# Tile 0's chosen pairs are turned inside the V convolution, z is cut into 16 pieces beside tokens 0 to 7, and V rows 0 to 3 are gathered behind the first six U rows

## What is computed

```python
p = h @ w_in                                     # RWKV-7 branch, gated delta (GDN) branch, gates
x1 = layer_norm(ALPHA * x + mix(p))              # recurrences over the tokens, then w_branch, w_out
q = x1 @ wq; s = q . subkeys                     # 8 heads x 2 halves x 128 keys
s1, i1 = top_k(s[:, :, 0], 16); s2, i2 = top_k(s[:, :, 1], 16)
sc, ci = top_k(s1[:, None] + s2[None, :], 16)    # 16 of 256 pairs in each head
expert = i1[ci // 16] * 128 + i2[ci % 16]        # 8 heads x 16 = 128 experts for each token
gate = softmax(sc)
ff = sum_k gate_k * gelu(u_tab[expert_k] . x1) * v_tab[expert_k]
y = layer_norm(ALPHA * x1 + ff)
```

## Time and profile before

| What | us |
|---|---|
| Median of 3 runs | 2156.04 (2153.06 to 2158.79) |
| The profiled execution's own time | 2147.0 |
| Its span in the profile | 2145.2 |
| Busy: PE, DVE, POOL, ACT | 1622.2, 1335.1, 1022.3, 398.1 |
| First U gather issued | 490.02 |
| Last V gather issued | 2123.56 |
| TensorE's mean granted clock, of full speed | 0.795 |

### The profile page before, as it was taken

How to read it: one execution, slowest core, us unless ns; L and a number is a source line. 1 busy time by engine, 2 the same in 40 slices (tenths; PEclk the granted TensorE clock), 3 DMA queues, 4 the chain that set the end, 5 groups by cost and what they waited for, 6 DMA issues and landing times. The chain is left out here.

```text
span 2145.2 us, 32147 instructions
## 1 busy us (share of the span) xinstructions
PE 1622.2 (76%) x12789; PEld 967.1 (45%) x12789; DVE 1335.1 (62%) x2994; ACT 398.1 (19%) x754; POOL 1022.3 (48%) x1093
## 2 busy tenths in 40 slices
PE   7998979899978795597887656988886656655564
PEld 7887866765655561165665302565552001100000
DVE  4286178785545458774545778655457865776745
ACT  1321332242222011122401201232012001000000
POOL 0000020004745455665545566655455777777774
PEclk9997999998989896598999756999887555555555
DMA  9214285657999999999999999999999999999996
GB/s 255 79 49 135 82 225 177 223 192 259 384 374 399 399 401 411 376 374 373 399 399 400 415 401 376 385 367 398 399 400 406 388 402 407 407 406 403 403 407 270
DMA packets 271256, 718.93 MB, mean 335 GB/s; under 512 B 29219, under 2 KB 77822, under 8 KB 270074
## 3 DMA queue, kind: packets, MB, share of 16 engines
q0 software_dynamic: 151904, 554.59, 66.7%
q1 hardware_dynamic: 116552, 161.44, 21.9%
q10 hardware_dynamic: 2650, 0.85, 0.2%
HBM read 695.58 MB, written 21.30 MB: 334 GB/s over the span
## 5 line engine op out<-in xcount | busy, mean ns | idle before, releaser
L2540 DVE CUSTOM_DVE_ANT_0 arena<-arena,ps 128x1024 f32<-128x1024 f32 x520 | 634.5, 1220 | 505.6 <-PE ps L2593 312.6
L2434 POOL DMA_INDIRECT arena<-peer_u_dram,arena x520 | 503.3, 968 | 480.5 <-DVE arena L2540 394.6
L2483 POOL DMA_INDIRECT arena<-peer_v_dram,arena x520 | 490.1, 942 | 163.8 <-issue 153.0
L2593 PE MATMUL ps<-arena 48*128 48x512 bf16 x1040 | 262.2, 498 | 321.5 <-DVE arena L2540 317.9
L1323 PE MATMUL ps<-arena 128*128 128x128 f32 (+1 forms) x3072 | 418.1, 292 | 91.3 <-DMA arena<-w_in_dram 35.9
L1323 PEld LDWEIGHTS ps<-arena 128*128 128x128 f32 x3072 | 382.8, 201 | 182.5 <-issue 121.0
L2608 PE MATMUL ps<-arena 128*32 128x512 f32 x2080 | 394.0, 841 | 23.1 <-DMA arena<-peer_v_dram,arena 22.8
L2593 PEld LDWEIGHTS ps<-arena 48*128 48x128 bf16 x1040 | 53.4, 97 | 633.2 <-DVE arena L2540 563.3
L2574 ACT ACTIVATE arena<-arena 128x4 f32<-128x4 f32 x130 | 26.8, 206 | 901.9 <-DVE arena L2540 901.5
L387 PE MATMUL ps<-arena 128*128 128x260 f32 (+1 forms) x704 | 131.3, 349 | 3.9 <-ACT arena L465 3.9
L387 PEld LDWEIGHTS ps<-arena 128*128 128x128 f32 x704 | 116.2, 193 | 17.9 <-ACT arena L465 4.0
(11 more groups left out here) (368 smaller groups left out, 1795.9 us busy)
## 6 DMA issues: line engine op xcount, KB each, us to landing
arena<-w_in_dram SPq DMA_DIRECT2D x40, 1024.0 KB, 13.0
...
arena<-peer_u_dram,arena POOLq DMA_INDIRECT x520
arena<-peer_v_dram,arena POOLq DMA_INDIRECT x520
...
```

The costliest lines, as they stand in the source:

```text
L2434: pool.indirect_dma_start(m["arena"][:, at:at + D], None, m["a"]["peer_u"][0], offsets(m, k)).then_inc(m["sem"](f"e_u{k % RU // UB}"), 16)
L2483: pool.indirect_dma_start(e["V"][j % RV], None, a["peer_v"][0], offsets(m, j)).then_inc(v_in[j % RV // BATCH], 16)
L2540: dve.tensor_tensor_reduce(u, u, ps[:, 0:2, :], 1.0, 0.0, ALU.mult, ALU.add, e["hp"][:, c:c + 1]).then_inc(sem("e_h"), 1)
L2593: mm = pe.matmul(ps[:, h, :], e["pick"][r, i:i + 1].to_broadcast([3 * GROUP, P]), e["xp"][r, g % 2, :], start=True, stop=True)
```

## The change

- `turn_chosen` and `take_chosen` of tile 0 leave z and become steps of their own at `TURN_AT` = -41, between the third and the fourth column tile of the V convolution. The first tail transpose, which writes the same banks, waits for the copies.
- In `choose`, for all tiles, the indices get a tag (16 places x 256) by one OR; stage 7 is then an XOR with the wanted tag and a minimum, two passes of 128 x 1024 where there were three, and two type casts go.
- For tile 0 the two remainders of x1 are taken by POOL, behind the spill of q, where DVE did them; the exponentials, the scale matrices of the convolution (`late_at("v", 0) + 1.5`) have new places on ACT.
- z: 16 pieces of two slices each, from -0.3 in steps of 0.5 (two pieces per token, tokens 0 to 7); its second slab lies in `ring[1]`, so that `ring[0]` is free once V is projected.
- POOL gathers V rows 0 to 3 right behind U rows 0 to 5. z's spill moves from place 8.5 to 12.5, V row 4 waits for it and for the stored tails.
- `BEGINS[1]` goes from 3.0 to 6.0, `TURN[0]` (the turn of tile 1's pairs) from 116 to 120.

```diff
@@ -143,7 +143,7 @@
-BEGINS = (-160.0, 3.0, 118.0, 244.0)
+BEGINS = (-160.0, 6.0, 118.0, 244.0)
@@ -687,6 +687,11 @@
+def late_place(ring, kind, h, number):
...
+    return ring[1] if (kind, h) == ("z", 1) else ring[number % SLOTS]
@@ -1279,7 +1284,7 @@
-        here = d["ring"][number % SLOTS] if once is None else once
+        here = late_place(d["ring"], kind, i, number) if once is None else once
@@ -1462,7 +1467,9 @@
-        if q:
+        if q and n == 0:
+            act.wait_ge(m["sem"]("first_left"), q)
+        elif q:
@@ -1561,6 +1568,9 @@
+        if n == 0:
+            dve.sem_inc(F_["left"], 1)
+            continue
@@ -1591,7 +1601,7 @@
-        yield at + CHOOSE_PACE[count] * (32 * half + 27) + 0.2
+        yield (slab_at(0, 23) + 0.3, EXP_AT)[half] if count == 0 else at + CHOOSE_PACE[count] * (32 * half + 27) + 0.2
@@ -1599,12 +1609,11 @@
...
...
-    iota = const(m, "iota16").unsqueeze(1).unsqueeze(1).to_broadcast(full)
-    keys = topf.rearrange("p (h q) k -> p h q k", q=2)
+    keys = keyed.rearrange("p (h q) k -> p h q k", q=2)
@@ -1637,7 +1646,9 @@
-            link(dve.tensor_copy(topf, topi))
+            if half == 0:
+                link(dve.tensor_scalar(tags, const(m, "iota16"), float(2 * NK), None, ALU.mult))
+            link(dve.tensor_tensor(keyed, topi, tags.unsqueeze(1).to_broadcast([P, 2 * CH, TK]), ALU.bitwise_or))
@@ -1653,17 +1664,15 @@
-            st.did(dve.tensor_scalar(pos[:, 0], place, 4, None, ALU.logical_shift_right))
-            st.did(dve.tensor_scalar(pos[:, 1], place, 15, None, ALU.bitwise_and))
+            st.did(dve.tensor_scalar(pos[:, 0], place, 4, 3840, ALU.logical_shift_left, ALU.bitwise_and))
+            st.did(dve.tensor_scalar(pos[:, 1], place, 8, 3840, ALU.logical_shift_left, ALU.bitwise_and))
...
-            link(dve.tensor_copy(posf, pos))
...
-            link(dve.tensor_tensor(one, posf[:, q].unsqueeze(3).to_broadcast(full), iota, ALU.is_equal))
-            link(dve.tensor_tensor(one, one, keys[:, :, q].unsqueeze(2).to_broadcast(full), ALU.mult))
+            link(dve.tensor_tensor(one, pos[:, q].unsqueeze(3).to_broadcast(full), keys[:, :, q].unsqueeze(2).to_broadcast(full), ALU.bitwise_xor))
...
-            link(dve.tensor_reduce(pair_ids[:, q], one, AXX, ALU.add))
+            link(dve.tensor_reduce(pair_ids[:, q], one, AXX, ALU.min))
@@ -1815,13 +1824,22 @@
+    d = front(m, 0)
+    for q in range(2):
+        m["fs"].wait(pool, 0, "part", q + 1)
+        if q:
+            pool.wait_ge(sem("first_left"), 1)
+        pool.tensor_tensor(d["left"], d["left"] if q else d["x1row"], d["parts"][:, q], ALU.subtract).then_inc(sem("first_left"), 1)
...
-    yield LAG - 0.5
+    pool.wait_ge(sem("b_mm"), late_number("v", 3))
+    for j in range(RV_FREE):
+        gather_v(m, pool, j)
+    yield LAG + RV_FREE - 0.5
@@ -1977,16 +1995,15 @@
-Z_AT = (begins(0) + LATE_AT["z"], -0.9, 0.1, 2.1)
-Z_TAKEN = (Z_AT[0] + 2.1, -0.3, 2.05, 4.05)
+TURN_AT, EXP_AT = -41.0, -43.2
...
-    return Z_AT[ct] if g == "z" else begins(0) + LATE_AT[g] + LATE_CT[g] * ct
+    return 2.0 * ct - 0.3 if g == "z" else begins(0) + LATE_AT[g] + LATE_CT[g] * ct
...
-    return Z_TAKEN[ct] if g == "z" else late_at(g, ct) + LATE_CT[g] * 0.95
+    return late_at(g, ct) + (1.55 if g == "z" else LATE_CT[g] * 0.95)
@@ -2004,8 +2021,11 @@
-            yield late_at(g, ct)
+            if g != "z":
+                yield late_at(g, ct)
...
+                if g == "z":
+                    yield late_at(g, ct) + 1.0 * h
@@ -2013,15 +2033,11 @@
-                    if g == "z" and ct > 1 and k % 2 == 0:
-                        yield late_at(g, ct) + 0.5 * (2 * h + k // 2)
-                    mm = pe.matmul(ps[:, bank(g, ct), 0:NL_], ring[number % SLOTS][:, k, ct * P:(ct + 1) * P], m["xT"][:, 4 * h + k, P:NP],
+                    if g == "z" and k == 2:
+                        yield late_at(g, ct) + 1.0 * h + 0.5
+                    mm = pe.matmul(ps[:, bank(g, ct), 0:NL_], late_place(ring, g, h, number)[:, k, ct * P:(ct + 1) * P], m["xT"][:, 4 * h + k, P:NP],
...
-            if (g, ct) == ("z", 0):
-                pe.wait_ge(sem("s_done"), 2)
-                pe.wait_ge(sem("sel_done"), 2)
-                turn_chosen(m, pe, front(m, 0))
@@ -2049,6 +2065,7 @@
+            pe.wait_ge(sem("sel_taken"), 2)
@@ -2058,6 +2075,19 @@
+def turned_pe(m, pe):
+    yield TURN_AT
+    pe.wait_ge(m["sem"]("s_done"), 2)
+    pe.wait_ge(m["sem"]("q_kout"), 2)
+    pe.wait_ge(m["sem"]("sel_done"), 2)
+    turn_chosen(m, pe, front(m, 0))
...
+def turned_act(m, act):
+    yield TURN_AT + 0.75
+    take_chosen(m, act, 0)
@@ -2085,8 +2115,6 @@
-                if ct == 0:
-                    take_chosen(m, act, 0)
@@ -2113,7 +2141,7 @@
-    yield late_at("v", 0) - 0.5
+    yield late_at("v", 0) + 1.5
@@ -2200,7 +2228,7 @@
-TURN = (116, 116, 116, 108)
+TURN = (120, 116, 116, 108)
@@ -2210,7 +2238,7 @@
-    m["e"]["junk"] = f["choose"]["one"].rearrange("p h i j -> p (h i j)")
+    m["e"]["junk"] = f["choose"]["one"].rearrange("p h i j -> p (h i j)").bitcast(F32)
@@ -2434,6 +2462,10 @@
+def gather_v(m, pool, j):
+    pool.indirect_dma_start(m["e"]["V"][j % RV], None, m["a"]["peer_v"][0], offsets(m, j)).then_inc(m["sem"](f"e_v{j % RV // BATCH}"), 16)
@@ -2463,7 +2495,6 @@
-    v_in = [sem(f"e_v{k}") for k in range(RV // BATCH)]
@@ -2473,14 +2504,13 @@
-        if j >= 0:
-            if j == 0:
+        if j >= RV_FREE:
+            if j == RV_FREE:
...
-            elif j == RV_FREE:
...
-            pool.indirect_dma_start(e["V"][j % RV], None, a["peer_v"][0], offsets(m, j)).then_inc(v_in[j % RV // BATCH], 16)
+            gather_v(m, pool, j)
@@ -2613,7 +2643,7 @@
-    pe.wait_ge(sem("sel_taken"), 2)
+    pe.wait_ge(sem("tail_out"), len(TAILS))
@@ -2663,7 +2693,7 @@
-            in_turn(recur_r_act(m, act, 0), recur_g_act(m, act, 0), front_act(m, act, 0), sample_act(m, act), late_act(m, act),
+            in_turn(recur_r_act(m, act, 0), recur_g_act(m, act, 0), front_act(m, act, 0), sample_act(m, act), late_act(m, act), turned_act(m, act),
@@ -2687,7 +2717,7 @@
-            in_turn(recur_r_pe(m, pe, 0), recur_g_pe(m, pe, 0), front_pe(m, pe, 0), sample_pe(m, pe), late_pe(m, pe),
+            in_turn(recur_r_pe(m, pe, 0), recur_g_pe(m, pe, 0), front_pe(m, pe, 0), sample_pe(m, pe), late_pe(m, pe), turned_pe(m, pe),
```

More of the change, by code:

```diff
@@ L155 @@
 PAIRS = WIDE * TK + (TK - WIDE) * NARROW
-CHOOSE = (("top", [P, 2 * CH, TK], F32), ("topi", [P, 2 * CH, TK], U32), ("topf", [P, 2 * CH, TK], F32), ("cand", [P, CH, PAIRS], F32),
-          ("one", [P, CH, TK, TK], F32), ("best", [P, CH, TK], F32), ("besti", [P, CH, TK], U32), ("pos", [P, 2, CH, TK], U32),
-          ("where", [P, CH, TK], U32), ("skip", [P, CH, TK], F32), ("posf", [P, 2, CH, TK], F32), ("pair_ids", [P, 2, CH, TK], F32), ("ex", [P, CH, TK], F32), ("exsum", [P, CH], F32),
+CHOOSE = (("top", [P, 2 * CH, TK], F32), ("topi", [P, 2 * CH, TK], U32), ("keyed", [P, 2 * CH, TK], U32), ("cand", [P, CH, PAIRS], F32),
+          ("one", [P, CH, TK, TK], U32), ("best", [P, CH, TK], F32), ("besti", [P, CH, TK], U32), ("pos", [P, 2, CH, TK], U32),
+          ("where", [P, CH, TK], U32), ("skip", [P, CH, TK], F32), ("tags", [P, TK], U32), ("room", [P, 7, TK], F32), ("pair_ids", [P, 2, CH, TK], F32), ("ex", [P, CH, TK], F32), ("exsum", [P, CH], F32),
           ("ids", [P, PH, TK], F32), ("gates", [P, PH, TK], F32))
@@ L1601, in choose @@
     sem = m["sem"]
-    (top, topi, topf, cand, one, best, besti, pos, place, skip, posf, pair_ids, ex, exsum, ids, gates) = (d["choose"][k] for k in (
-        "top", "topi", "topf", "cand", "one", "best", "besti", "pos", "where", "skip", "posf", "pair_ids", "ex", "exsum", "ids", "gates"))
+    (top, topi, keyed, cand, one, best, besti, pos, place, skip, tags, pair_ids, ex, exsum, ids, gates) = (d["choose"][k] for k in (
+        "top", "topi", "keyed", "cand", "one", "best", "besti", "pos", "where", "skip", "tags", "pair_ids", "ex", "exsum", "ids", "gates"))
     work = d["scores"][:, 8 * half:8 * half + 8]
     full = [P, CH, TK, TK]
-    iota = const(m, "iota16").unsqueeze(1).unsqueeze(1).to_broadcast(full)
-    keys = topf.rearrange("p (h q) k -> p h q k", q=2)
+    keys = keyed.rearrange("p (h q) k -> p h q k", q=2)
     pair = (2 * part, 2 * part + 1)
```

## The result

The changed kernel takes 2136.77 us (median, 2122.96 to 2148.89), the kernel before 2154.78 beside it: ratio 0.9917, 95% interval 0.989 to 0.9944, some 17.9 us (12 to 24) less. Two more series gave 0.9939 (0.9906 to 0.9971) and 0.993 (0.9906 to 0.9954). The profiled execution took 2128.82, its span 2127.0, which is 18.2 less than before.

The account below looks back on a forecast made before the run. Bytes were taken to bound the kernel from some 540 us on. The start's -6.3 and the selections' -1.5 summed to -7.8 us: profiled execution 2139.2, median 2148.2, 0.36% less, range 2140 to 2157.

Parts of the forecast that it names:

- What bounds the kernel: From some 540 us on, bytes at about 400 GB/s set the end, 2.60 us per token; a faster engine brings nothing.
- the hole of 530 to 540 us: DMA dip to 283 GB/s where tile 1's recurrence holds tokens up; forecast to come again with other tokens.
- DVE and the turn: Tile 0's selection up to the turn: pairs ready at 474.5, 12.8 us earlier; first U gather 480.8 for 490.02.
- POOL's subtractions: Tile 0's two remainders on POOL: 1.2 to 2.4 us each, costing DVE 0 to 4.9, taken as 0.5.
- the first rival: Pairs not ready when PE comes, DVE held by POOL's reads or slower integer passes: -3.4 us, 2152.6; chance 20%.
- Tokens 0 to 8: Loop's first steps: token 0 at 487.7, z's pieces set 3.10 us per token, token 8 at 511.1.
- The gain from the start: 6.3: At tile 1's recurrence: three tokens of bytes, 7.8 us, less 1.5 us for the same work running later.
- Selections of tiles 1 to 3: 0.5 us a tile, 1.5: DVE does 5.6 us less per tile, mostly beside a full DMA, so only 0.5 a tile counts, 1.5 in all.
- The fourth rival: DVE's relief counts half at the tile borders, 8.4 us in place of 1.5: 2141.3; chance 10%.
- The border of tiles 0 and 1: Second rival: the 7.9 us lost at that border double and give all back, 2156.1; chance 12%.
- z at the low clock: Third rival: all of z's pieces at 1.2 GHz cost 22.8 us, net +15, 2171; chance 6%.

Follow-up runs that it names:

- a_hold: The changed kernel with five subtractions on POOL put between the taken pairs and the first U gather; median 2146.5 us, ratio 0.9969 to the kernel before.
- a_left: The changed kernel with tile 0's two remainders of x1 back on DVE, POOL's subtractions and waits undone; median 2148.46 us, ratio 0.9973.
- b_begins: The kernel before with only `BEGINS[1]` 6.0 and `TURN[0]` 120; median 2150.91 us, ratio 0.9996.
- b_sel: The kernel before with only the new selection (tagged indices, XOR, minimum) in all tiles; median 2145.61 us, ratio 0.997.
- b_both: The kernel before with the new selection and tile 1 begun at 6.0, its pairs turned at 120; median 2147.25 us, ratio 0.9968.
- b_later: The kernel before with tiles 1, 2 and 3 each three tokens later (`BEGINS` 6, 121, 247; `TURN` 120 for tiles 0 to 2); 2133.0 us, ratio 0.9928.
- the doses: The changed kernel with stage 7's XOR made twice or three times for tiles 1 to 3 and the samples; 2142.51 and 2147.99 us, ratios 0.9961 and 0.9988.

## Why the prediction was too small

**What bounds the kernel: right for the start, wrong for stage 7.** Bytes do on the whole; what is gained at the first gather is still there at token 260 (a_hold). The step that failed is the sentence behind it, that in a stretch with the DMA busy "a faster engine brings nothing": beside the selections the DMA is busy and DVE sets the tokens all the same, and a microsecond off DVE there was worth about half of one. The second step that failed is the hole of 530 to 540 us, which did not come again. Both are taken in turn below.

**DVE and the turn: right.** Pairs ready at 474.87 for 474.5, although V began 1.64 us later; no wait before the turn; first gather 34.07 us behind V's start where the forecast's 480.8 - 445.77 gives 35.0. The XOR took 1.23, the minimum 1.21 to 1.22, as forecast.

**POOL's subtractions: right, and more needed than the forecast knew.** Each took 1.99, in the bounds of 1.2 and 2.4. The 0.5 us charged to DVE is not there: the searches beside the first subtraction run from 449.78 to 452.12, the same ones beside nothing from 459.82 to 462.17. The relief was counted as the 1.1 of the second pass, and the pairs were ready when the sum said. By a_left the same subtractions on DVE would have cost 6.1, as with the scale matrices moved between ACT's parts DVE would have waited for ACT; that the two moves depend on each other is not in the forecast. The Trainium skill ("SBUF — State Buffer", Who interferes with whom) would have DVE instructions with two SBUF operands stand for the whole of a POOL instruction; the searches that ran beside POOL read one tensor each, so no row here tests that rule, and the first rival, which it fed, did not come. The page "GPSIMD Engine Reference" (3.1) gave an estimate of 2.25 us; the trace has 1.99.

**Tokens 0 to 8: right in steps.** Token 8's product stands 66.5 us behind V's start, the forecast's 511.1 gives 65.3; the one z pair at 4.45 for 2.85 is more than that difference, and token 0 came 0.5 sooner than forecast. The clock was 0.50 from 490.4 to 493.8 us, inside that pair and behind PE's stand of 3.31 us. U row 13 at 516.36 and V row 4 at 519.16 stand 1.0 and 1.1 later than forecast, counted so.

**"The gain from the start: 6.3": too small.** The leads of the changed kernel at token 28 are 8.9, 8.4, 7.0, and at token 108, with the second half of tile 1's selection still ahead, 10.4, 10.6, 8.4: mean 9.8, 3.5 more. The failed sentence is that the hole of 530 to 540 us comes again. It did not (412 GB/s for 283); at 404 GB/s the missing bytes of that hole are 3.0 us by my estimate, nearly the whole difference. It went with the place of tile 1's recurrence, and not with the clock. b_begins has the kernel before's turn and z, tile 1 three tokens later, and a clock of 0.50 from 510 to 527 us, and there is no hole in it:

```profile
520.00:530.00 10.00, 7.93 (x94) 4.94 (x89) 8.09 (x17) 2.70 (x5) 7.48 (x8) 0.65 1.02 411
530.00:540.00 10.00, 9.38 (x161) 7.11 (x158) 9.38 (x17) 1.20 (x2) 7.25 (x8) 1.00 1.03 406
```

b_sel, with tile 1 where it was, has it:

```profile
530.00:540.00 10.00, 9.75 (x206) 6.58 (x203) 6.21 (x13) 2.16 (x5) 7.56 (x9) 1.00 0.86 286
```

In b_both, which has the shift too, a shallow one stands later (some 320 GB/s at 543 to 553 us), so how far the shift removes it is known from few profiles. The shift alone leads by 5.7 at token 108 in b_begins and 5.8 in b_later; so much of the 9.8 may be its own. The forecast had it only as the three tokens that it counted as bytes. The recurrence also ran at a higher clock: it stood at 0.50 for 20.5 us before (511.1 to 531.5) and for 3.4 us after. That the dense z pieces kept the clock up is what these profiles suggest; no run has tried it alone. Nor was the earlier turn tried without the shift of tile 1.

**"Selections of tiles 1 to 3: 0.5 us a tile, 1.5": mis-sized by a factor of six to seven for tiles 1 and 2.** In place of 1.0 at token 260 it is 7.3 by b_sel and 5.9 by the doses; the changed kernel gains 7.3 from token 108 to 260 (17.1 - 9.8). I had judged by the DMA's average and by DVE's average (63 of 80 us busy), and both hide stage 7, in which DVE goes without idle time for some eight tokens. The fourth rival had the mechanism and nearly the size, half of DVE's relief, 8.4 for three tiles, with a chance of 10%.

So the sum at token 260 is 9.8 + 7.3 = 17.1 in place of 6.3 + 1.0 = 7.3. Behind it come 9 us of chance, in both kernels: the three ratios give 17.9, 13.1 and 15.1 us, the profiled pair, in which neither has the long stretch at half clock, 18.2.

**The rivals.** The border of tiles 0 and 1 did not get worse: 405 GB/s at 860 to 900 us for 377, 356 for 351 after it. z at the low clock cost the 1.6 us of one pair, not the rival's 22.8. The measured time lies nearest to the fourth rival's 2141.3, and still 4.5 below it.
